# Stacked delta-rule chunks: output product and output copy ahead of the state product

## The reference, cut to what matters

```python
def step(s, inp):
    r_t, w_t, k_t, v_t, kk_t, a_t = inp
    sa = jnp.einsum("bhvk,bhk->bhv", s, -kk_t)
    s = (s * w_t[:, :, None, :] + sa[..., None] * (kk_t * a_t)[:, :, None, :]
         + v_t[..., None] * k_t[:, :, None, :])
    return s, jnp.einsum("bhvk,bhk->bhv", s, r_t)
```

## Time and profile before

| | us |
|---|---|
| median of 3 runs | 2458.35 (2457.72 to 2460.19) |
| the profiled execution | 2451.51 |
| its span in the trace | 2448.9 |
| chunk loop, layer 0 | about 312 to 485 |
| chunk loop, layer 1 | about 1178 to 1351 |
| experts of layer 1 | about 1460 to the end |

### The profile page before, as it was taken

One profiled execution on the slowest core, in us unless ns is written; L12 is line 12 of the kernel. 1 busy time (PEld: TensorE's weight loads), 2 busy tenths in 40 slices (PEclk: granted clock), 3 DMA queues, 4 the chain that ended last, 5 costly groups with the idle time before them and its releaser, 6 DMA issues.

```text
span 2448.9 us, 43502 instructions
## 1 busy us (share of the span) xinstructions
PE 2269.3 (93%) x17639; PEld 1722.5 (70%) x17639; DVE 1586.7 (65%) x1871; ACT 1289.9 (53%) x1556; POOL 166.2 (7%) x162
## 2 busy tenths in 40 slices
PE   5999878798999999999677999999999999999997
PEld 3446457645888786556566678888888888888886
DVE  3574557524333332675464379898989898989897
ACT  3341456503222233433465267777777777777774
POOL 0000044300000000000353000000000000000000
PEclk9999989998999999999799989999999999999998
DMA  7122700143232226221000859999999999999997
GB/s 294 64 86 69 271 6 4 58 186 98 91 103 89 84 84 232 69 87 52 2 21 4 327 206 367 346 368 336 370 338 372 343 365 342 364 340 369 341 367 259
DMA packets 234852, 500.43 MB, mean 204 GB/s; under 512 B 9446, under 2 KB 78332, under 8 KB 227676
## 3 DMA queue, kind: packets, MB, share of 16 engines
q1 hardware_dynamic: 232544, 484.24, 55.0%
q10 hardware_dynamic: 2172, 14.20, 1.5%
HBM read 492.12 MB, written 6.29 MB: 204 GB/s over the span
## 4 chain that ended last, share of the span: by engine, by line
PE 89%; DVE 4%; ACT 3%; issue 2%; POOL 1%; DMA 1%; ACTq 0%; DVEq 0%; POOLq 0%
PE ps L603 18%; PE ps L604 17%; PE ps L605 17%; PE ps L692 11%; PE ps L596 8%; PE ps L885 6%; PE ps L631 2%; PE ps L1180 1%; PE ps L1223 1%; PE ps L1030 1%; PE ps L1082 1%; PE ps L1189 1%; POOL tail L2415 1%; PE ps L942 1%; PE ps L920 1%
## 5 line engine op out<-in xcount | busy, mean ns | idle before, releaser
L2319 DVE TENSOR_TENSOR weight_parts<-front,weight_parts 128x2048 fp32r<-128x2048 f32 x336 | 767.7, 2289 | 101.9 <-ACT weight_parts L1686 98.0
L1686 ACT ACTIVATE weight_parts<-front 128x2048 fp32r<-128x2048 f32 x336 | 643.6, 1919 | 252.7 <-PE ps L605 252.6
L603 PE MATMUL ps<-weight_parts,token_parts 128*128 128x512 f32 x1344 | 533.2, 397 | 1.8 <-issue 1.8
L604 PE MATMUL ps<-weight_parts,token_parts 128*128 128x512 f32 x1344 | 525.0, 391 | 0.0
L605 PE MATMUL ps<-weight_parts,token_parts 128*128 128x512 f32 x1344 | 524.6, 390 | 0.0
L603 PEld LDWEIGHTS ps<-weight_parts,token_parts 128*128 128x128 f32 x1344 | 253.0, 188 | 56.1 <-DVE weight_parts L2319 4.5
L605 PEld LDWEIGHTS ps<-weight_parts,token_parts 128*128 128x128 f32 x1344 | 252.9, 188 | 54.9
L692 PE MATMUL ps<-front,tail 128*128 128x512 f32 (+3 forms) x704 | 282.2, 557 | 6.5 <-ACT front L1389 4.4
L604 PEld LDWEIGHTS ps<-weight_parts,token_parts 128*128 128x128 f32 x1344 | 253.3, 188 | 49.2
L692 PEld LDWEIGHTS ps<-front,tail 128*128 128x128 f32 (+1 forms) x704 | 132.3, 190 | 147.3 <-issue 139.5
L603 PE MATMUL ps<-token_parts,weight_parts 128*128 128x512 f32 x528 | 207.5, 393 | 11.6 <-DVE token_parts L2202 6.5
(11 more groups left out here) (268 smaller groups left out, 2405.1 us busy)
## 6 DMA issues: line engine op xcount, KB each, us to landing
front<-in_exp_w SPq DMA_DIRECT2D x345, 1024.0 KB, 7.0
tail<-in_ffn_w SPq DMA_DIRECT2D x30, 1024.0 KB, 5.1
tail<-in_ada_w SPq DMA_DIRECT2D x27, 1024.0 KB, 8.7
tail<-in_w_in SPq DMA_DIRECT2D x24, 1024.0 KB, 5.1
front<-in_ada_w SPq DMA_DIRECT2D x21, 1024.0 KB, 10.6
tail<-in_w_out SPq DMA_DIRECT2D x8, 1024.0 KB, 5.1
parked_x<-front ACTq DMA_DIRECT2D x2, 2048.0 KB, 11.2
front<-parked_x ACTq DMA_DIRECT2D x2, 2048.0 KB, 8.3
```

The costliest lines, as they stand in the source:

```text
L603: mm(view, a_hi, b_hi, start=start, stop=False)
L604: mm(view, a_lo, b_hi, start=False, stop=False)
L1686: f_(whi[k % PARTS], at(A_RING2 + (k % RING2) * SLOT2, SLOT2), ACT.Copy).then_inc(cnt["act"].sem, 1)
L2319: ins = v.tensor_tensor(wlo[k % PARTS], at(A_RING2 + (k % RING2) * SLOT2, SLOT2), whi[k % PARTS], ALU.subtract)
```

## The change

On TensorE the second part of Y moves ahead of level(4), and S moves behind level(4). On VectorE `outputs(n)` moves from behind doubled(4) to ahead of level(4), and `state(n)` from ahead of level(4) to behind doubled(4). On GpSimd masks 1 and 2 of chunk `n + 2` move ahead of `decayed(n)`. No instruction is added or dropped, and no DMA moves.

```diff
--- before.py
+++ after.py
@@ -997,17 +997,17 @@
                         doubled(3, n + 1)
                     if seq_:
                         banks.released(pe, ("U", l, n))
-                    if seq_ and n < STEPS - 1:
-                        banks.released(pe, ("KB", l, n))
-                        small(("S", l, n), lambda d, cc, h: KB[d][:, cc, h, :], lambda d, cc, h: VU[d][:, cc, h, :],
-                              P_SEQ, straight)
-                    if inv:
-                        level(4, n + 1)
                     if y:
                         if n > 0:
                             after_straight(n, 1)
                         small(("Y", l, n), lambda d, cc, h: VU[d][:, cc, h, :],
                               lambda d, cc, h: GHT[n % 3][d][:, h, cc, 1, :], P_OUT, straight, begin=n == 0)
+                    if inv:
+                        level(4, n + 1)
+                    if seq_ and n < STEPS - 1:
+                        banks.released(pe, ("KB", l, n))
+                        small(("S", l, n), lambda d, cc, h: KB[d][:, cc, h, :], lambda d, cc, h: VU[d][:, cc, h, :],
+                              P_SEQ, straight)
                     if inv:
                         doubled(4, n + 1)
                         keys_turned(n + 1)
@@ -2123,13 +2123,13 @@
                         level(3, n + 1)
                         attention_root()
                         doubled(3, n + 1)
-                    if 0 <= n < STEPS - 1:
-                        state(n)
+                    if n >= 0 and with_y(l, n):
+                        outputs(n)
                     if inv:
                         level(4, n + 1)
                         doubled(4, n + 1)
-                    if n >= 0 and with_y(l, n):
-                        outputs(n)
+                    if 0 <= n < STEPS - 1:
+                        state(n)
                     if inv:
                         level(5, n + 1)
                     if pre:
@@ -2431,10 +2431,12 @@
                     if pre:
                         level_mask(n + 2, 0)
                         begun(n + 2)
+                        level_mask(n + 2, 1)
+                        level_mask(n + 2, 2)
                     if 0 <= n < STEPS - 1:
                         decayed(n)
                     if pre:
-                        for b in range(1, LEVELS):
+                        for b in range(3, LEVELS):
                             level_mask(n + 2, b)
 
             def feed_forward():
```

## The result

| | before | changed |
|---|---|---|
| median | 2458.72 (2447.73 to 2460.19, 6 runs) | 2442.51 (2436.74 to 2448.39, 6 runs) |
| profiled execution | 2451.51 | 2447.52 |
| its span | 2448.9 | 2445.3 |

The ratio is 0.9945, with a 95% interval of 0.9927 to 0.9963; a second comparison on another occasion gave 0.9950 (0.9930 to 0.9969). That is 12 to 14 us less, and the medians of the table differ by 16.2. The forecast was 10.8 less and 2447.5.

What follows compares the result with a forecast made beforehand. TensorE was taken to idle in the chunk loops waiting for outputs, with ScalarE binding next. A gain of 11.76 us less 1.0 for instruction stalls gave 10.8, from 2458.35 to 2447.5 us, with a range of 2442 to 2454.

Steps and rivals of the forecast that it cites:

- Part 1: TensorE's ten 1.54 us waits of the key transposes for outputs go; ScalarE takes some back, leaving a gain of 11.76 us.
- Rival A: ScalarE doesn't bind, so the ten waits go in full: 15.4 us less, or 2443.0; chance 0.08.
- Part 2: Y and S change places around level(4) on TensorE, with cover of the same length: cost 0.
- Parts 3 and 4: VectorE's state behind doubled(4): cost 0, at most 2 us; GpSimd's two masks ahead of the decay: cost 0.
- Part 5: Without the 1.54 us pause TensorE may stall more for late instructions: 1.0 us taken, bounds 0 and 6.1.
- Rival B: Instruction supply takes half of the gain: 5.7 us less, or 2452.7; chance 0.17.
- Rivals C and D: C: the wait moves to VectorE's queue, about 2458, chance 0.11. D: TensorE runs dry every changed iteration, 2471.6, chance 0.04.

Runs made afterwards that it cites:

- experiment d: The changed kernel with the three copies of the started inverse done by GpSimd in place of ScalarE; 0.9934 of the kernel before.
- f: The changed kernel with S and the state addition back ahead of level(4), right behind Y and the outputs; 0.9963 of the kernel before.
- b: The changed kernel with GpSimd's old order, the decay of the state first and then masks 1 to 5; 0.9936 of the kernel before.
- again: The changed kernel once more with no edit, for a second profile; 0.9950 of the kernel before.
- l: The changed kernel with the third tile of output weights loaded only when Y of chunk 7 is there; 0.9968 of the kernel before.
- e: The changed kernel with VectorE taking Y out behind doubled(4) again, ahead of the state; 0.9988 of the kernel before.
- before again: The kernel before once more with no edit, for a second profile; ratio 1.0006, profiled execution 2457.42 us.

## Why the prediction was right, point by point

**Part 1, the wait of the keys, was right in mechanism and size.** Ten distances sum to 76.4 us before and to 64.5 and 64.8 in the two profiles of the changed kernel: 11.9 and 11.6 less, where 11.76 was forecast. Against the second profile of before, 78.1, it is 13.6 and 13.3 less, since that one was longer in chunk 0 and, at the lower clock, in chunk 1. The value taken from layer 1's chunks without outputs, 6.57, came out as 6.52 to 6.60 in most; chunk 0 of layer 0 had 6.75 in both. For chunk 4 of layer 0, 6.74 was forecast and 6.54 and 6.89 came; for chunk 6, about 5.9, and it was 5.89 and 6.06 to 6.08. That ScalarE is what binds was only argued from its idle time; experiment d shows it. In the step after chunk 5 the changed trace shows it directly: TensorE waits 1.44 us at 456.78 for ScalarE's line 1567, within the distance of 6.53. Rival A is out by the same rows, and by them alone: its 15.4 us lie inside the interval of the first comparison (9.1 to 17.9), and the forecast's 10.8 do too.

**Part 2 was right where there are outputs** (f shows what it would have cost to leave S in front), **and off by a little where there are none.** There 0 was taken, with 0.1 as the bound. TensorE in such a step of layer 1:

```profile
1235.34 0.69 PE L885 MATMUL ps<-tail 64*64 64x64 f32 x32 [0.80 <-DVE tail L2054]
1237.13 2.40 PE L885 MATMUL ps<-tail 64*64 64x64 f32 x96 [1.10 <-DVE tail L2062]
1239.47 1.09 PE L942 MATMUL ps<-front 128*128 128x128 f32 x8
```

```profile
1236.10 0.45 DVE L2061 STREAM_TRANSPOSE tail<-ps 128x256 f32<-128x256 f32 x1
1236.47 0.41 DVE L2062 STREAM_TRANSPOSE tail<-ps 128x256 f32<-128x256 f32 x1
```

The wait ahead of level(4) is 1.10 us, not 0.8. doubled(3) ends at 1236.03; the transposes take 0.78 us, to 1236.88, and TensorE starts 0.25 behind them, where the forecast had 0.70 (it took the start of VectorE's next instruction for their end) and 0.1. From the start of doubled(3) to the keys it is 4.13 us, against 3.90 before (1236.30 to 1240.20). In two profiles of each kernel such steps have 3.84 to 3.90 us in seven of eight before and 4.13 in five of eight now; the other four, 5.27 to 6.27, had the lower clock. So it is 0.2 to 0.3 in each of four steps.

**Parts 3 and 4 were right**: no new wait at values_turned, doubled(4) or R for VectorE or GpSimd. The 0.33 us that GpSimd waits for the state was not foreseen and is harmless, as b shows.

**Part 5 is the term that I can't confirm.** 1.0 us was taken for more stalls once the pause is gone. R to doubled(4) sums to 139.5, 142.4 and 140.5 in three profiles with the pause, and to 143.4, 143.1, 142.0 and 137.9 in four without (changed, again, l, b): means of 140.8 and 141.6. Of the 0.8 between them, about half are the steps without outputs (part 2, which e has as well). The stalls alone, of 0.2 us and more and without those of 0.46 to 0.50, sum to 7.2, 7.8 and 5.3 with the pause and to 7.3, 6.8, 9.7 and 4.0 without. So the pause bought nothing that these runs can show; the forecast without this term, 11.76, is nearer to the 12 to 14 measured. No row gave the size of 1.0, so that the sum still came out close owes nothing to this term. Its sign of being wrong, "issue" before line 885 growing beyond 3 us, did not come: 11.0 us before, 13.0 and 10.4 in the two changed profiles. That the stalls come with instruction packets, as I took it, is supported by their timing, not proved by an experiment. The Trainium skill ("Runtime: NRT & Kernel Launch", "Instruction fetch mechanics") has fetching hidden; these loops show 4 to 10 us of such stalls in each of those seven profiles, which it does not account for.

**The sum.** The measured median, 2442.51, lies 5.0 us below the forecast, below the 2443 to 2451 given for the likeliest case, and only 0.5 us inside the range of 2442 to 2454. That it lies inside is partly luck; the mechanism does not rest on it, but on the distances and on idle time that fell by 13.0 to 15.3 us. The forecast took it that the length of the loops doesn't depend on the execution, which was wrong: they were 346.2 us in the trace of before that it was read from and 351.8 in the next. So the signs given for the loops came out unevenly. Layer 0's loop was to be 8 to 9 us shorter and layer 1's about 3; they were 4.1 and 2.9 shorter in the first pair of profiles, 12.2 and less than 0.1 in the second. The span of the changed kernel's first profile was only 3.6 us less, because 3.4 us more lay outside the loops (2.7 of them ahead of the first) and R to doubled(4) was 3.9 us longer, with 1.0 us less idle time but 10.9 us at 1.2 GHz in place of 3.4. The runs, and the second profiles of each, put the gain at 12 to 16 us.

Rival B (supply takes half) would have been 5.7 less: excluded by both intervals, whose lower ends are 9.1 and 7.6 us (0.9963 and 0.9969). Rivals C and D fall with them.

## What to carry to other kernels

Where an engine waits for the last user of a buffer, look for an iteration in the same trace that lacks that user: it shows what binds next, and here it gave the gain per step to 0.1 us in most steps. A wait of 1.5 us was worth 0.9 where the next engine in line had only 0.85 of air, and all of it in chunk 6, where that engine itself waited for the same event; on average 1.2. To size a change of half a per cent, take two profiles of each side and compare the idle time of the busy engine, not only lengths: the loops of one kernel differed by 5.6 us between executions, 4.0 of them in the busy time of the same matmuls.

## What was not expected of the hardware

- A wait on a semaphore that was long satisfied held up TensorE's queue by 39 ns each (35.0 us over 896).
- A 1 MB transfer at 314 to 410 GB/s in a stretch of dense matmuls went with a TensorE stall of up to 2.50 us, which ended 1.39 us after a packet of instructions; five of eleven profiles with the transfer have such a stall, of 1.3 us or more.
- The granted clock fell to 1.2 GHz for 3.4 to 13.7 us within the loops, in most cases right behind idle time of TensorE (2.50 us ahead of 1269.8 in before, 1.53 ahead of 381.6 in before again, 0.81 ahead of 1272.5 in changed), and at other places in each execution of one kernel. From before to before again, 7.1 us more at 1.2 GHz went with 4.0 us more busy time, the larger part of the 5.6 us by which the loops differ.
